# PEER rows of the sample: four slots side by side in PSUM partition quarters, and a fold at the end

## The reference, cut to what matters

```
e = (i1[pos // 16] * 128 + i2[pos % 16])          # 8 heads x 16 experts for each row
u = take(u_tab, e);  act = gelu(einsum('nkd,nd->nk', u, xb)) * gate
v = take(v_tab, e);  out = einsum('nk,nkd->nd', act, v)
x = x + out;  y = rmsnorm(x, final_g)
```

## Time and profile before

| | us |
|---|---|
| median of 3 runs (lowest, highest) | 2125.84 (2120.86, 2131.23) |
| span of the profiled execution, first to last instruction | 2123.7 |
| PE busy | 1870.6 (88%) |
| DVE busy | 1479.7 (70%) |
| ACT busy | 838.9 (40%) |
| POOL busy | 645.4 (30%) |

### The profile page before, as it was taken

The page is one execution under the profiler, slowest core; times in us unless marked ns, Lnnn a source line. Parts: engine busy times, 40 slices in busy tenths (PEclk is TensorE's granted clock), DMA queues, the critical chain, the costliest instruction groups (busy, mean ns, idle before and its releaser), DMA issues.

```text
span 2123.7 us, 23959 instructions
## 1 busy us (share of the span) xinstructions
PE 1870.6 (88%) x8010; PEld 1214.2 (57%) x8010; DVE 1479.7 (70%) x3271; ACT 838.9 (40%) x2343; POOL 645.4 (30%) x549
## 2 busy tenths in 40 slices
PE   8999999889988899999899779898998877777776
PEld 7888998656555567777566455664454432222321
DVE  4163631398877678789998368898878667667664
ACT  2523111243523476458535134445423333333332
POOL 0000000134332333333434124344433434444442
PEclk9999999899999999999999889999998999999999
DMA  6343225799999999999999989999999999999997
GB/s 230 107 150 129 90 99 180 285 377 354 379 407 378 418 408 368 408 371 370 397 338 386 409 326 375 349 370 370 380 409 418 421 398 421 421 421 421 422 384 302
DMA packets 128132, 724.62 MB, mean 341 GB/s; under 512 B 16336, under 2 KB 23120, under 8 KB 57872
## 3 DMA queue, kind: packets, MB, share of 16 engines
q0 software_dynamic: 78336, 570.46, 67.1%
q1 hardware_dynamic: 49056, 150.49, 19.1%
q10 hardware_dynamic: 624, 2.23, 0.3%
HBM read 714.08 MB, written 8.52 MB: 340 GB/s over the span
## 4 chain that ended last, share of the span: by engine, by line
PE 48%; DMA 25%; DVE 17%; ACT 5%; issue 3%; POOL 1%; DVEq 0%; POOLq 0%; ACTq 0%
DMA arena<-in_uv,arena 18%; PE ps L1068 14%; PE ps L1016 8%; PE ps L738 6%; DVE arena L1938 6%; PE ps L794 5%; DMA arena<-in_stream 3%; PE ps L934 3%; PE ps L885 2%; PE ps L875 2%; PE ps L884 2%; DMA arena<-in_w_q 2%; DMA arena<-in_w_out 2%; DVE arena L1804 1%; POOL arena L1502 1%
## 5 line engine op out<-in xcount | busy, mean ns | idle before, releaser
L1502 POOL DMA_INDIRECT arena<-in_uv,arena x544 | 644.3, 1184 | 1179.8 <-PE ps L1068 783.9
L1068 PE MATMUL ps<-arena 128*128 128x512 f32 (+1 forms) x1660 | 796.6, 617 | 121.2 <-ACT arena L1463 121.0
L1938 DVE CUSTOM_DVE_ANT_0 arena<-arena 128x1024 f32<-128x1024 f32 x544 | 659.6, 1222 | 235.3 <-DMA arena<-in_uv,arena 232.9
L1068 PEld LDWEIGHTS ps<-arena 128*128 128x128 f32 (+1 forms) x1660 | 293.6, 190 | 492.4 <-issue 290.9
L1477 ACT ACTIVATE gelu_d<-dots 128x2 f32<-128x2 f32 x272 | 55.8, 205 | 761.5 <-DVE dots L1938 760.7
L1016 PE MATMUL ps<-arena 128*128 128x294 f32 (+1 forms) x1152 | 291.3, 414 | 14.7 <-DMA arena<-in_stream 9.8
L1016 PEld LDWEIGHTS ps<-arena 128*128 128x128 f32 x1152 | 219.3, 191 | 88.9 <-DMA arena<-in_stream 12.8
L934 PE MATMUL ps<-arena 128*128 128x128 f32 (+1 forms) x1024 | 140.7, 298 | 28.4 <-DMA arena<-in_w_a 13.7
L934 PEld LDWEIGHTS ps<-arena 128*128 128x128 f32 x1024 | 135.8, 206 | 45.8 <-DMA arena<-in_w_a 15.7
L738 PE MATMUL ps<-arena 128*128 128x256 f32 x640 | 141.6, 384 | 3.5 <-DVE arena L1525 3.0
L1463 ACT ACTIVATE arena<-ident,share 128x128 f32<-128x128 f32 x383 | 136.8, 397 | 7.1
(11 more groups left out here) (282 smaller groups left out, 2007.0 us busy)
## 6 DMA issues: line engine op xcount, KB each, us to landing
arena<-in_stream SPq DMA_DIRECT2D x144, 512.0 KB, 5.0
arena<-in_w_a SPq DMA_DIRECT2D x32, 512.0 KB, 8.1
arena<-in_w_out SPq DMA_DIRECT2D x32, 512.0 KB, 10.0
arena<-in_w_q SPq DMA_DIRECT2D x32, 512.0 KB, 7.8
arena<-in_uv,arena POOLq DMA_INDIRECT x544, 11.0
arena<-spill SPq DMA_DIRECT2D x2, 1920.0 KB, 13.9
arena<-in_x_prompt SPq DMA_DIRECT2D x4, 512.0 KB, 5.3
arena<-in_ln_g SPq DMA_DIRECT2D x4, 512.0 KB, 8.8
```

The lines of the kernel that those rows point to most:

```text
L1068: mm = pe.matmul(ps[0:L, half, :], diag[on_pe(k) % NDIAG][:, 0:L], ring[k % SLOTS][:, D + half * 512:D + (half + 1) * 512], start=False, s ...
L1502: pool.indirect_dma_start(out=ring[kk % SLOTS], out_offset=None, in_=a["uv"], in_offset=bass.IndirectOffsetOnAxis(ap=idx[:, kk:kk + 1], ax ...
L1938: ins = dve.tensor_tensor_reduce(ring[s][:, 0:D], ring[s][:, 0:D], n2p if t == NTILE else n2[t % 2], 1.0, 0.0, ALU.mult, ALU.add, dots[k / ...
```

## The change

In the sample's stage PE adds four slots at once in the order of `add_four`. Slot j goes to its own quarter of PSUM partitions, 32 (j mod 4) to 32 (j mod 4) + 31, of the same two banks. The number of matmuls for a slot stays two. PE waits until the diags of all four slots are there, issues the eight matmuls of the group (first half of all four, then second half), and the last of them raises `slot_free` by 4. At the end ACT copies all 128 partitions of both banks into `fins[0]`, PE multiplies them by `fold` into banks 2 and 3 (two matmuls), and ACT copies the 32 partitions out again. Two semaphores at the start of the kernel are merged into others (`sp_log` into `sp_abs`, `sp_sum` into `sp_x`), with the same instructions waiting for the same instructions.

```diff
@@ PE
+            def add_four(k):
+
+                pe.wait_ge(diag_ready, on_pe(k) + QUARTERS)
+                for half in range(2):
+                    for j in range(k, k + QUARTERS):
+                        quarter = slice(TS * (j % QUARTERS), TS * (j % QUARTERS) + TS)
+                        mm = pe.matmul(ps[quarter, half, :], diag[on_pe(j) % NDIAG][:, 0:TS],
+                                       ring[j % SLOTS][:, D + half * 512:D + (half + 1) * 512],
+                                       start=j % P in (1, 2, 3), stop=j >= NS - QUARTERS)
+                mm.then_inc(slot_free, QUARTERS)
@@
                     if k % P == 0:
                         open_sum(k // P)
-                    if not on_dve(k):
+                    if k >= NTILE * P:
+                        if k % QUARTERS == QUARTERS - 1:
+                            add_four(k - (QUARTERS - 1))
+                    elif not on_dve(k):
                         add_row(k)
+
+            pe.wait_ge(quads_copied, 1)
+            for half in range(2):
+                mm = pe.matmul(ps[0:TS, 2 + half, :], fold[:, :], fins[NTILE % 2][:, half * 512:(half + 1) * 512],
+                               start=True, stop=True)
+            mm.then_inc(quads_folded, 1)
@@ ACT, finish_sums
-                if not mixed(t):
+                if t == NTILE:
+                    act.wait_ge(slot_free, on_pe(NS))
+                    act.wait_ge(y_out[t % 2], uses(t // 2))
+                    act.copy(fin, ps[:, 0:2, :].rearrange("p b n -> p (b n)")).then_inc(quads_copied, 1)
+                    act.wait_ge(quads_folded, 1)
+                    acc = ps[0:L, 2:4, :].rearrange("p b n -> p (b n)")
+                    act.copy(fin[0:L, :], acc).then_inc(fin_copy, 1)
+                elif not mixed(t):
                     act.wait_ge(slot_free, on_pe(min((t + 1) * P, NS)))
@@ ACT and DVE, start of the kernel
-            act.activation(spl[:, :], spl[:, :], ACT.Ln, bias=1.0).then_inc(sp_log, 1)
-            act.activation(beta[:, :, :], bg[:, :, 0:H], ACT.Sigmoid).then_inc(sp_log, 1)
+            act.activation(spl[:, :], spl[:, :], ACT.Ln, bias=1.0).then_inc(sp_abs, 1)
+            act.activation(beta[:, :, :], bg[:, :, 0:H], ACT.Sigmoid).then_inc(sp_abs, 1)
-            dve.wait_ge(sp_log, 2)
+            dve.wait_ge(sp_abs, 4)
             dve.scalar_tensor_tensor(out=spx[:, :], in0=spx[:, :], scalar=0.0, in1=spl[:, :],
-                                     op0=ALU.max, op1=ALU.add).then_inc(sp_sum, 1)
-            dve.wait_ge(sp_sum, 1)
+                                     op0=ALU.max, op1=ALU.add).then_inc(sp_x, 1)
+            dve.wait_ge(sp_x, 2)
```

More of the change, by code:

```diff
@@ L234, in trunk_program @@
         sp_abs = sem("sp_abs")
-        sp_log = sem("sp_log")
-        sp_sum = sem("sp_sum")
         g_ready = sem("g_ready")
@@ L342, in trunk_program @@
         fin_step = sem("fin_step")
+        quads_copied = sem("quads_copied")
+        quads_folded = sem("quads_folded")
         fin_copy = sem("fin_copy")
```

## The result

Ten runs of each kernel: median 2138.56 us (2131.39 to 2140.94) for the changed kernel, 2128.62 us (2120.86 to 2136.45) for the one before. The ratio on record is 1.0037, with a 95% interval of 1.0020 to 1.0054: 7.9 us slower, between 4.3 and 11.5 (the two medians by themselves lie 9.9 us apart). The 7.9 us are within the 0.5% (10.6 us) that I counted as the same, though clear of zero, and the interval reaches just past it.

A forecast was written before the change was run, and what follows sets the result against it. DMA gathers, not PE, were taken to bound the sample's stage. Start 0.4, ring 1, last group 0, copy 1.0 and fold 3.7 sum to +6.1 us, a forecast of 2132 us, counted as the same, range 2124 to 2153.

The forecast's parts named there:

- What bounds the stage: Sample's stage, slots 512 to 543: the DMA gathers bound it, not PE, so less PE work cannot make it faster.
- PE4: PE's time for the sixteen passes of a four-slot group: 3.6 us, four abreast at half clock, bounds 1.8 and 14.5.
- Start, +0.4: From the end of x2 to the stage's first freed-slot gather: 0.4 us later, bounds -1.3 and +5.4.
- The ring, +1 (0 to +4): Eight gather buffers reused through the stage: waiting for four freed slots costs 1 us, bounds 0 and +4.
- the pessimistic price: Restarting the ring's gathers takes 15.0 us where 12.0 was put; two groups lose 1.3 us, three times, +4.
- The end, +4.7: After the last landing: last group 0, copy of 128 partitions +1.0, fold +3.7 us.
- The copy: At the end, ACT's extra copy of 128 partitions: +1.0 us, since the copy of 32 remains.
- The fold: At the end, four passes in one quarter, one after the other: +3.7 us at half clock, 1.95 at full.
- Two of the signs: Signs of a wrong forecast: last landing after about 2111.5 us; DMA share visibly under 1 once per group.
- no overlap: Rival: a group's passes do not run side by side; +18 to +26 us, middle 2148 us; chance 0.20.
- two abreast at the full clock: Rival: two quarters' passes run at once; +9 us, 2135 us (+18 at half clock); chance of two abreast 0.20.
- Full clock four abreast: Rival: PE keeps clock 1.00 despite the gaps, four quarters at once; +1.6 us, 2127 us; chance 0.10.

The follow-up runs named there:

- coarse: Kernel before, only POOL's wait changed so gathers wait until a whole group of four slots is free: 96.8 us x2 to end (before 86.8), ratio 1.0036.
- pairs: Changed kernel with slots added and freed in twos instead of fours, copy and fold kept: 91.1 us x2 to end, ratio to before 1.0006.
- fold_only: Kernel before with only the new end (copy, fold, copy, on 32 partitions) and the merged semaphores: 90.8 us x2 to end, ratio to before 1.0017.
- warm_more: Changed kernel with eight filler matmuls before each group (six before the second, none before the first): 90.7 us x2 to end, ratio to before 1.0015.
- one_quarter: Kernel before with groups of four slots all added into one quarter, no copy or fold: 108.1 us x2 to end, ratio to before 1.0082.
- slot_order: Changed kernel with the two loops of add_four exchanged, each slot's passes together in program order: 96.1 us x2 to end, ratio to before 1.0039.

## Why the prediction was right, and where not

The forecast was 2132 us and +6.1 us, the same within 0.5%, in a range of 2124 to 2153. Measured: 2138.6 and +7.9 by the ratio, +7.4 by the traces. The median lies above the forecast also because the kernel before has 2128.6 in ten runs where three gave 2125.8.

**What bounds the stage.** Right. PE's sixteen passes fell from 7.2 us to 3.6 and nothing came back for it, and coarse and pairs show that the steps in which slots come free decide: in fours they cost as much without the quarters, in twos they cost nothing with them.

**PE4 = 3.6 us, four abreast at the half clock.** Right in both halves, with the clock at 0.50 in the groups: 3.2 to 3.6 us. The Trainium skill, "TensorE: Matmul & The Clock Gate", section Part 3, gives 2.38 times for three column slices. Here the runs give more for four: 7.05 us in one quarter against 1.92 us in four quarters, 3.7 times.

**Start, +0.4.** The number came out, +0.45, but not by its terms. I had x2 at 3.62 us and the group right behind it. In the trace x2 takes 2.20 us, since the granted clock was 0.84 there, and PE then waits 1.37 us for the diags of the group, which I had put at nothing. The two nearly cancel, by luck. Nor are the 0.45 us clear of scatter: fold_only, which frees slot by slot, has +0.4 as well.

**The ring, +1 (0 to +4).** This is the term that was mis-sized: +3.7. I put 12.0 us from a group's first gather to its fourth landing and kept 15.0 as the pessimistic price. In the changed kernel it is 15.1 to 15.7 in every group. With 6.2 to 6.8 us from the last landing to that gather, two groups take 21.3 to 22.2 us where the DMA alone wants 19.9. That holds twice in the stage, not three times, and the start of the stretch is 0.6 us shorter: 2.0 + 2.3 - 0.6 = 3.7. By these rows PE4 would be hidden only up to about 1.9 us, not up to 5.3; that is an estimate, which warm_more does not test well. Part of the missing 3 us is shown by one_quarter, where the queue is quite empty: the first dot comes 5.5 us after its gather's issue, not the 4.5 that I had built up, and the second 3.1 to 3.7 after it instead of 2.49. Another part shows in the stretches: the DMA moves only half as much (208 GB/s from 2096.5) already 2 us before the last row has landed (dot at 2098.72), so the queue counted in rows was less deep than it looked. Why slot 536 then takes until 2103.5 is not settled, and warm_more has shown that with the same start it can come 2.4 us sooner.

**The end, +4.7.** The copy was right (1.0), the last group too (3.68 instead of 3.63). The fold took 1.92 us instead of 3.7, since the granted clock was 1.00 from the end of the last group on. In four other kernels with the same end 3.62 us came out; in slot_order the clock was still 0.50 there. The price is right for either level, and nothing here says which one comes.

Two errors went in opposite directions, +2.7 in the ring and -1.7 in the fold, so it is luck that the sum is nearer than its terms. Two of the signs by which I had said the forecast would be wrong did appear. The last dot comes 77.2 us after x2, which is 2114.1 on the scale of the kernel before, where I had drawn the line for the last landing at 2111.5, and the DMA's share is visibly under 1 (0.84) before a group lands. Both point at the ring.

**The rivals.** One_quarter puts a number on no overlap, 21 us and some 24 to 26 with the copy and the fold. The +9 us that I gave for two abreast at the full clock only come out with the start and the fold at the half clock. Two abreast did not occur even in slot_order. Full clock four abreast: only with filler work.

## What to carry to other kernels

Work that is moved off an engine which does not bound the stage brings nothing, and how it is grouped can cost: here half of the loss comes from freeing the ring's buffers in fours, by itself, as one changed wait in POOL shows. Count the cover of such a ring from a landing, by rows of the trace for a queue that has just run low (they varied by 2 us here), not by the latency of a full queue or of a single transfer built up from parts. Where passes are added into separate partition quarters, the join at the end (two copies with a matmul between, 3 us here) must be paid back by PE time that is on the critical path.

## What was not expected of the hardware

PE's clock can rise when it is of no use. The stretches of the changed kernel (columns as above):

```profile
2060.00:2062.00 2.00, 1.95 (x12) 0.20 (x4) 0.07 (x1) 0.00 (x0) 0.00 (x0) 0.50 1.04 434
2062.00:2064.00 2.00, 0.00 (x0) 0.00 (x0) 1.16 (x2) 0.74 (x4) 1.71 (x1) 0.93 0.99 418
2064.00:2066.00 2.00, 0.00 (x0) 0.00 (x0) 1.23 (x2) 0.48 (x2) 1.43 (x2) 0.92 0.98 389
2066.00:2068.00 2.00, 0.00 (x0) 0.00 (x0) 1.15 (x1) 0.00 (x0) 1.39 (x2) 0.50 0.97 381
```

The group runs at 0.50 until 2062, the clock stands at 1.00 for most of the next 4 us in which PE does nothing, and is back at 0.50 before the next group at 2069.5. The other surprise is slot_order: a column quarter's passes start though several earlier ones of another quarter are still waiting, with all four quarters at work, as inferred above, in the first 0.16 us.
